# Head pairs for the sink layer, reordered dilated steps and single-pass suffix sums in a four-layer hybrid decoder

## The reference, cut to what matters

```python
# sb: z = q k / 8, strictly causal
sp = where(causal, softplus(z), 0.0)
after = lax.cumsum(sp, axis=3, reverse=True) - sp
a = where(causal, exp(log_sigmoid(z) - after), 0.0)
o = a @ v
# swa: window 128, 2 kv heads for 16 q heads, rotary on q and k
m = maximum(s.max(-1), sink)
e = exp(s - m)
den = e.sum(-1) + exp(sink - m)
o = (e / den) @ v
# dil: head groups (128,1), (512,4), (2048,16), rotary, a softmax for
# each group, merged per head by the denominators
```

## Time and profile before

| what | value |
|---|---|
| median of 3 runs | 2350.6 us (2345.4 to 2352.5) |
| the profiled execution | 2351.3 us, its span 2349.4 us |
| TensorE busy | 2304.9 us, 98% |
| VectorE, ScalarE busy | 1313.4 us, 1100.7 us |
| mean granted TensorE clock | 0.982 |
| chain of work that ended last | 93% TensorE |

### The profile page before, as it was taken

How to read it: one execution, slowest core, us unless ns; L and a number is a source line. 1 busy time by engine, 2 the same in 40 slices (tenths; PEclk the granted TensorE clock), 3 DMA queues, 4 the chain that set the end, 5 groups by cost and what they waited for, 6 DMA issues and landing times.

```text
span 2349.4 us, 27306 instructions
## 1 busy us (share of the span) xinstructions
PE 2304.9 (98%) x11172; PEld 1890.0 (80%) x11172; DVE 1313.4 (56%) x1658; ACT 1100.7 (47%) x1395; POOL 18.1 (1%) x53
## 2 busy tenths in 40 slices
PE   8999999999999899999999999989999999999999
PEld 7888778888888578887888878868887888778887
DVE  5455355556455555456545766655456545446455
ACT  5444555445444445445444444355445444555443
POOL 0000000000000000000000000000000000000000
PEclk9999999999999679999999999999999999999999
DMA  8555336556654127555655634526655664436553
GB/s 290 179 185 183 99 119 222 187 176 202 201 188 154 62 78 228 187 193 172 210 175 162 195 127 144 162 90 208 206 179 171 212 194 149 150 109 215 184 178 114
DMA packets 212941, 401.51 MB, mean 171 GB/s; under 512 B 12368, under 2 KB 30928, under 8 KB 212688
## 3 DMA queue, kind: packets, MB, share of 16 engines
q1 hardware_dynamic: 212816, 399.76, 52.2%
HBM read 398.66 MB, written 1.05 MB: 170 GB/s over the span
## 4 chain that ended last, share of the span: by engine, by line
PE 93%; DVE 3%; ACT 2%; DMA 2%; issue 1%; POOL 0%; SPq 0%; ACTq 0%; DVEq 0%; POOLq 0%
PE ps L1064 27%; PE ps L1066 27%; PE ps L1065 27%; PE ps L1107 5%; DVE wl L751 1%; PE ps L1193 1%; PE ps L1223 1%; PE ps L1247 1%; DMA raw<-in_ffn_w_in 1%; PE ps L1258 1%; ACT wh L463 1%; PE ps L1331 1%; PE ps L1350 1%; PE ps L1250 0%; PE ps L1248 0%
## 5 line engine op out<-in xcount | busy, mean ns | idle before, releaser
L751 DVE TENSOR_TENSOR wl<-raw,wh 128x1024 fp32r<-128x1024 f32 x730 | 867.4, 1222 | 524.0 <-ACT wh L463 519.6
L463 ACT ACTIVATE wh<-raw 128x1024 fp32r<-128x1024 f32 x730 | 753.7, 1059 | 588.5 <-PE ps L1066 415.8
L1064 PE MATMUL ps<-wh,xh 128*128 128x512 f32 (+1 forms) x2320 | 888.6, 383 | 5.6 <-DVE xl L758 4.8
L1065 PE MATMUL ps<-wl,xh 128*128 128x512 f32 (+1 forms) x2320 | 878.3, 379 | 0.0
L1066 PE MATMUL ps<-wh,xl 128*128 128x512 f32 (+1 forms) x2320 | 878.3, 379 | 0.0
L1064 PEld LDWEIGHTS ps<-wh,xh 128*128 128x128 f32 x2320 | 439.7, 190 | 88.1 <-DVE xl L758 6.5
L1066 PEld LDWEIGHTS ps<-wh,xl 128*128 128x128 f32 x2320 | 439.2, 189 | 81.6
L1065 PEld LDWEIGHTS ps<-wl,xh 128*128 128x128 f32 x2320 | 439.4, 189 | 77.8
L1064 PE MATMUL ps<-wh,hth 128*128 128x512 f32 x736 | 289.2, 393 | 0.2 <-DVE htl L764 0.2
L1066 PE MATMUL ps<-wh,htl 128*128 128x512 f32 x736 | 286.7, 390 | 0.0
L1065 PE MATMUL ps<-wl,hth 128*128 128x512 f32 x736 | 286.6, 389 | 0.0
(11 more groups left out here) (92 smaller groups left out, 972.9 us busy)
## 6 DMA issues: line engine op xcount, KB each, us to landing
raw<-in_ffn_w_in SPq DMA_DIRECT2D x352, 512.0 KB, 4.7
raw<-in_ffn_w_out SPq DMA_DIRECT2D x176, 512.0 KB, 4.4
raw<-in_dil_w_in SPq DMA_DIRECT2D x72, 512.0 KB, 4.5
raw<-in_sb_w_in SPq DMA_DIRECT2D x48, 512.0 KB, 4.1
raw<-in_ple_w_gate SPq DMA_DIRECT2D x32, 512.0 KB, 4.7
raw<-in_sb_w_out SPq DMA_DIRECT2D x16, 512.0 KB, 3.8
gb<-in_ln_g SPq DMA_DIRECT2D x12, 512.0 KB, 4.0
gb<-in_ln_b SPq DMA_DIRECT2D x12, 512.0 KB, 4.9
```

The source lines that it names most:

```text
L463: act.activation(wh[:, u % RING, :], raw[:, u % RAWS, :], ACT.Copy).then_inc(hi_done, 1)
L751: dve.tensor_tensor(wl[:, u % RING, :], raw[:, u % RAWS, :], wh[:, u % RING, :].bitcast(F32), ALU.subtract).then_inc(lo_done, 1)
L1064: pe.matmul(out_, a_h, b_h, start=start, stop=False)
L1065: pe.matmul(out_, a_h, b_l, start=False, stop=False)
```

## The change

- **swa**: kv is loaded, rotated and transposed first, then the q of half 0, then the q of half 1. The attention is one pipeline of 8 steps, a step being two heads on both token tiles. The two heads of a score matmul pair use the two halves of the array in turn, and in the value product they write the two halves of the partitions. The negated sink is copied as an extra column beside each row of scores, so one exponential with accumulation takes it in. The normalizing is two `tensor_tensor` with the reciprocals broadcast. One evacuation serves a step. The q of half 1 is rotated after steps 0 and 1, transposed at step 2. Four units of the output projection run in steps 5 to 7 and behind the loop.
- **dil**: VectorE does the splits up to `b + 16` and normalize 2 before it copies v of group 2; half output 0 moves from step 4 to before step 2; the splits of `b + 17` to `b + 20` stand in steps 3 to 6 on both engines.
- **sb**: scores of both heads before their masks; `soft` rounds its result to fp32r as a high part and subtracts for a low part (in `hth`, `htl`); `cum` uses them with fp32r copies of `lower` and `ones`. The outputs lie in banks 0 and 1. Half 1's fills are two units of v and two of the output projection.
- Banks of the output projection and of the next stage's transposes change with it (`y_bank`, `x_bank`), and the first four units of it are loaded column half by column half for sb and swa.

```diff
@@ ScalarE, swa
+                def exps(s):
+                    act.wait_ge(s_done.sem, s_done.at(i, s))
+                    for m in range(2):
+                        for t in range(NT):
+                            w, n = swa_keys(t, 1), 4 * s + 2 * m + t
+                            ins = act.activation(ssc[:, s % 3, m, w], ssc[:, s % 3, m, w], ACT.Exp, bias=nmx[:, 0, n:n + 1], scale=-1.0,
+                                                 accum_out=nmx[:, 1, n:n + 1])
+                    ins.then_inc(e_done.sem, 1)
...
+                    evacuate(s)
+                    if s == 1:
+                        copy_t("swa", i, "q", 1, 0)
+                    if s == 4:
+                        half_out(0)
+                    if s >= 6:
+                        to(u0, 11 + s)
@@ ScalarE, sb
+                    logs(hh, 0)
+                    logs(hh, 1)
+                    to(u0, b + 16)
+                    if hh == 1:
+                        half0_out(i)
+                    weights(hh, 0)
+                    weights(hh, 1)
+                    to(u0, b + 17)
+                    logs(hh, 2)
+                    to(u0, b + 18)
+                    logs(hh, 3)
+                    to(u0, b + 19)
+                    weights(hh, 2)
+                    weights(hh, 3)
+                    to(u0, b + 20)
@@ VectorE, dil
                     normalize(hh, 1)
+                    to(u0, b + 16)
+                    normalize(hh, 2)
                     tokens("dil", "v", i, hh, 2)
+                    if hh == 1:
+                        half0_out(i)
                     scores(hh, 3)
-                    to(u0, b + 16)
-                    for s in range(2, STEPS):
+                    scores(hh, 4)
+                    for s in range(3, STEPS):
                         normalize(hh, s)
                         if s + 2 < STEPS:
                             scores(hh, s + 2)
-                        if (hh, s) == (1, 4):
-                            half0_out(i)
-                    if hh == 1:
-                        to(u0, b + 18)
+                        if s <= 6:
+                            to(u0, b + 14 + s)
@@ VectorE, swa
+                    dve.tensor_copy(ssc[:, s % 3, :, P:SW:2 * P + 1], nsink[:, 2 * s:2 * s + 2].unsqueeze(2).broadcast_to((P, 2, NT)))
...
+                    own(dve.reciprocal(nmx[:, 3, 4 * s:4 * s + 4], nmx[:, 1, 4 * s:4 * s + 4]))
+                    for t in range(NT):
+                        p_ = ssc[:, s % 3, :, swa_keys(t, 0)]
+                        ins = dve.tensor_tensor(p_, p_, nmx[:, 3, 4 * s + t:4 * s + 4:2].unsqueeze(2).broadcast_to((P, 2, (t + 1) * P)),
+                                                ALU.mult)
...
+                for s in range(STEPS):
+                    normalize(s)
+                    if s == 5:
+                        half_out(0)
+                    if s + 2 < STEPS:
+                        scores(s + 2)
+                    if s < NT:
+                        second_q(s)
+                    if s == NT - 1:
+                        dve.sem_inc(tok_done.sem, 1)
+                    if s >= 6:
+                        to(u0, 11 + s)
@@ VectorE, sb
+                def soft(hh, h):
+                    dve.wait_ge(ln_done.sem, ln_done.at(i, hh, h))
+                    own(dve.scalar_tensor_tensor(ssp[:, h % 2], zpair(h), 0.0, sw[:, h % 2], ALU.max, ALU.add))
+                    own(dve.tensor_copy(sph[:, h % 2], ssp[:, h % 2]))
+                    dve.tensor_tensor(spl[:, h % 2], ssp[:, h % 2], sph[:, h % 2].bitcast(F32), ALU.subtract).then_inc(sp_done.sem, 1)
...
+                    soft(hh, 0)
+                    to(u0, b + 16)
+                    soft(hh, 1)
+                    if hh == 1:
+                        tokens("sb", "v", i, 1, 0)
+                        half0_out(i)
+                    to(u0, b + 18)
+                    soft(hh, 2)
+                    to(u0, b + 19)
+                    soft(hh, 3)
+                    to(u0, b + 20)
@@ TensorE, swa
+                run(col_items(bank_of("swa", "kv", 0), 256) + q0[0:2], True, before=opening(i, 1))
+                run(q0[2:3], False)
+                pe.wait_ge(v_done.sem, v_done.at(i, 0, 0))
+                head_t("swa", i, "kv", 0, 0)
+                run(q0[3:4] + q1[0:2], False)
                 head_t("swa", i, "q", 0, 0)
+                run(q1[2:3], False)
+                pe.wait_ge(th_done.sem, th_done.at("q", i, 0, 0))
+                z(0)
+                run(q1[3:4], False)
+                z(1)
+                for s in range(STEPS):
+                    if s == 2:
+                        head_t("swa", i, "q", 1, 0)
+                        tr(s)
+                        pe.wait_ge(th_done.sem, th_done.at("q", i, 1, 0))
+                        z(s + 2)
+                    elif s < STEPS - 1:
+                        if s + 2 < STEPS:
+                            z(s + 2)
+                        tr(s)
+                    else:
+                        tr(s)
+                    if s:
+                        av(s - 1)
+                    if s == 5:
+                        pe.wait_ge(tl_done.sem, tl_done.at("o", i, 0))
+                        run([y[0]], False)
+                    if s == 6:
+                        run([y[2]], False)
+                pe.wait_ge(s_done.sem, s_done.at(i, STEPS - 1))
+                run([y[1]], False)
+                av(STEPS - 1)
+                run([y[3]], False)
@@ TensorE, sb
+                def cum(hh, h):
+                    pe.wait_ge(sp_done.sem, sp_done.at(i, hh, h))
+                    for m in range(2):
+                        for of in (sph, spl):
+                            pe.matmul(zpair(h)[:, m, :], lower_r[:], of[:, h % 2, m, :], start=False, stop=False, skip_group_check=True)
+                    for m in range(2):
+                        for of in (sph, spl):
+                            ins = pe.matmul(zpair(h)[:, m, P:2 * P], ones_r[:], of[:, h % 2, m, 2 * P:3 * P], start=False,
+                                            stop=of is spl, skip_group_check=True)
+                    ins.then_inc(cum_done.sem, 1)
...
+                        fill = [v[2], v[3], y[0], y[2]]
...
+                    run(fill[0:2], False)
+                    cum(hh, 0)
+                    cum(hh, 1)
+                    pe.wait_ge(v_done.sem, v_done.at(i, hh, 0))
...
+                    av(hh, 0)
+                    z(hh, 2)
+                    av(hh, 1)
+                    z(hh, 3)
+                    if hh == 1:
+                        pe.wait_ge(tl_done.sem, tl_done.at("o", i, 0))
+                    run(fill[2:3], False)
+                    cum(hh, 2)
+                    run(fill[3:4], False)
+                    cum(hh, 3)
```

More of the change, by code:

```diff
@@ L45 @@
 NJ = FF // BLK
+SW = 3 * P + 2
+STEPS = 2 * PAIRS
 DIL = ((128, 1), (512, 4), (2048, 16))
@@ L48 @@
 DW = 4 * P
-STEPS = 2 * PAIRS
 CONST = {}
@@ L195, in by_token, with swa_tile, swa_keys, swa_o @@
             return of.rearrange("p c t m -> p c (t m)").rearrange("p c (w k) -> p c k w", k=NT)
+        def swa_tile(t):
+            return slice(t * P, (1 + 2 * t) * P)
+        def swa_keys(t, sink):
+            return slice(t * (P + 1), t * (P + 1) + (t + 1) * P + sink)
+        def swa_o(hh):
+            return ps[:, 2 * hh:2 * hh + 2, :].rearrange("p b (c t m) -> p (b c) t m", c=2, t=NT)
+        def y_bank(i, t, c):
+            kind, l = stages[i][0:2]
+            if kind == "mix" and mixer_of(l) != "dil":
+                return (4 if c else {"sb": 2, "swa": 0}[mixer_of(l)]) + t
+            return 4 + 2 * t + c
+        def x_bank(i, t, c):
+            after_swa = i and stages[i - 1][0] == "mix" and mixer_of(stages[i - 1][1]) == "swa"
+            return 6 + c if after_swa and t == 0 else 2 * t + c
         def const(name):
@@ L283, in build_program @@
                             th_done.note(what, i, hh, g)
-                            if mixer_of(l) != "dil" and (mixer_of(l), hh) != ("swa", 1):
+                            if mixer_of(l) == "sb":
                                 t_ready.note(what, i, hh, g)
@@ L523, in copy_t @@
                 dst = kT[:, g] if what != "q" else qT[:, hh if kind == "swa" else g]
+                pair = head_bank(kind, what, hh)
                 for t in range(NT):
@@ L721, in _ @@
                         act.preload_act_table(ACT.Exp)
-                    dil(i, u0) if mixer_of(l) == "dil" else mix(l, i)
+                    {"sb": sb, "swa": swa, "dil": dil}[mixer_of(l)](i, u0)
                 else:
@@ L1323, in z, with dil @@
+            def dil(i):
                 def z(hh, s):
@@ L1521, in _ @@
                 elif kind == "mix":
-                    mix(l, i)
+                    {"sb": sb, "swa": swa, "dil": dil}[mixer_of(l)](i)
                 else:
```

582 lines of the change are left out of this document (208 added, 374 removed).

## The result

The kernel after took 2326.7 us in the median (2323.4 to 2327.9), the one before, measured beside it, 2351.1 us: a ratio of 0.989, 95% interval 0.988 to 0.991. It is faster, by 24 us instead of the 55 forecast, and lies above the range. The profiled execution took 2326.9 us, its span 2325.0. Three single executions of 5.8, 6.2 and 11.7 ms among the later runs are left out of the medians.

The account below looks back on a forecast made before the run. TensorE, busy 98% of the span, was taken as the bound, at half clock in swa's head loop. Savings of 38 (swa), 14 (dil) and 3 (sb) sum to 55: 2351.3 to 2296 us, range 2277 to 2318.

Parts of the forecast that it names:

- step (a): swa, before the first scores: weight units and transposes take 27.5 us, with rotating kv and q on VectorE beside them.
- steps (b) to (d): swa after its opening: pair loop 36.8 us, tail 20.1, then a fall to half clock costing some 2 plus 4.
- a step with a split: dil loop: 3.5 us of VectorE against TensorE's 3.13 in such a step, costing 1 to 1.5 us per half.
- The gains counted: dil: shorter transpose waits, no half-output or end-of-stage wait, less slow clock, earlier first keys; sum 18.7 us before costs.
- the closing gap: dil, end of stage: 3.9 us wait from six weight splits left after the last pair; moving them into steps removes it.
- the 3.3 us waits of the transposes: dil, each half: transposes 2 wait 3.35 us for normalize 2 behind two weight splits; their absence would show the forecast right.
- The paired order of scores: sb: lets only one matmul of a pair overlap, 0.15 us by 16 pairs, 2 us saved.
- fourth rival: sb: single-pass suffix sums are not cheaper, 30 us worse than taken, kernel 2326 us; chance 0.06.
- sum 1 comes 1.1 to 1.9 late: sb, every half: first suffix sum delayed 1.1 to 1.9 us, second about 1.9, by longer softplus and splits on VectorE.
- second rival: sb: all eight gaps drop the clock, 1.8 us each, 14 us lost, kernel 2310 us; chance 0.12.
- third rival: Whole kernel: everything holds, clock included, saving 44 + 17 + 10 us, kernel 2280 us; chance 0.14.
- the fifth: sb: VectorE's late sums pull whole pair loops to 1.2 GHz, 23 us each, 2388 us with all four; chance 0.04.

## Why the prediction was wrong

**The bound, and swa: right in the main.** Half clock in a light single-head loop was the thing to read. The stage came to 92.5 us (forecast 90). The pair in steady state was shorter than priced, 2.57 us instead of 3.0, with the two normalizing products together 1.03 us, and VectorE without a gap. The clock did as forecast: 0.57 in the early pairs and 1.00 later, in these windows of the kernel after:

```profile
790.00:802.00 12.00, 9.53 (x50) 6.73 (x50) 10.23 (x36) 5.78 (x20) 0.00 (x0) 0.57 0.00 1
802.00:815.00 13.00, 11.38 (x92) 7.58 (x92) 11.24 (x49) 12.31 (x41) 0.00 (x0) 1.00 0.01 1
```

Against that stood step (a): "Rotating kv and q on VectorE lies beside it, as keys come first" failed. Keys first means that VectorE's place in the stream of splits decides when the keys exist, and it stood in a split whose unit had not landed: 4.06 us. With a clock of 0.87 from 749 to 774 us, the first scores came 34.5 us after the first kv unit (749.03 to 783.50), where step (a) had 27.5. All the rest took some 5 us less than steps (b) to (d). That the total came within 2.3 us is in part luck.

**Dil: the failed step is "a step with a split is 3.5 us of VectorE (2.3 and 1.2) against TensorE's 3.13, 1 to 1.5 per half".** Adding up one engine's load says nothing of a ring over three engines. In series, transposes 1.1, evacuation 0.9 and split 1.1 on ScalarE, split 1.1 and reciprocal and normalize 1.1 on VectorE, are 5.3 us from durations that the trace before also had; 5.40 was measured. The gains counted were mostly real: without the in-loop splits the stage is 286.8 us at clock 1.00, 15 under before, where the gains alone (18.7, less 1 for the values) were to give 17.7. What was wrong was the price of moving splits into the steps, 19 us, priced at 2 to 3; and the closing gap that it was to buy off does not come back without it. Of the prediction's own signs, the closing gap did go, but the 3.3 us waits of the transposes did not.

**Sb: two errors of opposite sign.** "The paired order of scores lets only one matmul of a pair overlap, 0.15" was mis-sized: 1.12 us a pair, 7 times that. The mask products had kept two heads' 64-row products apart; side by side they cover each other wholly (the wide products of two heads take 0.54 us from start to start, as those of one head do alone). The Trainium skill, "TensorE: Matmul & The Clock Gate", Part 3, Packing small matmuls, says that products in different row groups of the array run at the same time; 2.33 against 1.21 us agrees. The suffix sums were sized well, 1.10 us against 1.2, so the fourth rival did not come.

The other: "sum 1 comes 1.1 to 1.9 late and sum 2 about 1.9 late" was right in place and too small: 2.3 to 3.1 us each, in eight of eight places, 20.9 us where its figures make 12 to 15. It was also netted wrongly. Against the 12 to 15 stood 10 us of savings and only 3.3 us of such waits in the kernel before, so the 3 us saved did not follow, unless the y units hid the rest. Two waits of 2.5 us for the second half's queries were in no term. And the slow clock behind the gaps, which the text held open as its second rival at 1.8 us a gap, came: the order without the gaps gave back 12.0 us of busy time, 1.5 a gap. In all TensorE was idle 27.4 us in the two stages, where the kernel before had 3.9, and busy 16.0 us less. That second rival was 2310, and with dil's 17 it makes the 2327 measured, but this is luck: it had sb lose 11 us, and sb lost 7.5, with 15 us or so of unforeseen savings from the scores set against waits that were longer than priced. The third rival did not come. Nor did the fifth: the stages' mean clock was 0.94, not half, since the fills between brought the clock back.

**Sum.** 2.3 (swa), 17 (dil), 10.5 (sb) and 0.7 in the first FFN, which nothing touched, make 30.5 of the 30.7 us between 2296 and 2326.7. The 2.3 lies within swa's scatter from run to run (89.7 to 92.5). The range was too narrow because its ends took the forecast price of each step with its uncertainty, and for dil no rival asked who waits for whom in a step with a split.

## What to carry over

Before an operation is moved into a loop, write down the whole round that it joins: which engine hands it to which, and what next step stands behind it. If its two halves lie on two engines and the loop's own work alternates between the same two, shift one half by a step. And put whatever TensorE is waiting for ahead of work that only has a later date (here the weight splits), before judging any other edit: the worth of a shorter product on TensorE had another sign in another order.

## What the hardware showed that was not expected

- After a wait of 2.5 us in sb the granted clock was 0.50 (1.2 GHz), then mixed (0.71 over 4 us) before it was 1.00 again. But waits of this length do not do it each time. In dil the wait of 2.21 us before 1371.54 was followed by transposes of 1.97 us instead of 1.09, the 3.29 us before 1383.22 by transposes of 1.09.
- The same swa code ran at a mean clock of 0.94 or 0.98, 2.2 us apart. Stages with such gaps scatter by 1.6 to 4.1 us from run to run; at clock 1.00 both sb stages repeated within 0.1 us (121.9 to 122.0 in six stages of three kernels).
- The rounding copy of 768 elements took 0.56 us and the subtraction of two such inputs 0.96. The Trainium skill, "VectorE: DVE Perf Modes", The perf-mode tier table, gives single-source fp32 operations on SBUF twice the rate of two-input ones; the trace agrees in direction, with a ratio of 1.7 for these two.
